# A conformer-like block with 32 experts on one core: the gating bias added by matmul instead of by VectorE, the convolution in eight columns per tap instead of four, one matmul group moved ahead of another

## The chip, the cores and the metric

The kernel runs on one core of a Trainium2 chip. The core's engines work side by side: TensorE (PE: matmuls; its weight loads are listed as PEld), VectorE (DVE), ScalarE (ACT), GpSimd (POOL), and SyncE (SP), which here only issues loads of weights. The metric is the device time of one execution in microseconds (us), lower is better.

## The reference

256 tokens of 1024 features pass through a first block and then through two layers of a second one. The change lies in the token mixer of the first block:

```
z = h @ w_in + b_in
a_val, a_gate, sgu, g_a, g_b = split(z)
ya = causal_depthwise_conv(a_val * sigmoid(a_gate), conv_w, conv_b)      # 31 taps per feature
ya = silu(layer_norm(ya)) @ w_a + b_a
u, v = split(gelu(sgu))
mixed = einsum('gij,bnjgc->bnigc', w, layer_norm(v)) + b_s[g, i]         # 8 groups, blocks of 128 tokens
yb = (u * mixed) @ w_b + b_b
y = (sigmoid(g_a) * ya + sigmoid(g_b) * yb) @ w_out + b_out
```

Behind it stand a layer norm, a mixture of 32 experts (4 per token, all 32 experts' weights are read), and the second block.

## The kernel before

**Tiles.** An activation that is feature-major has its features on the partitions as 8 columns `m` of 128, each with 256 tokens. It is held in `area`, which is cut into eleven pieces (`feat(i)`, `tok(i)`). A matmul group fills one of 8 PSUM banks; feature-major groups `q` = 0 to 3 hold columns 2q and 2q+1. Groups get their banks in turn, and a group's bank must have been emptied of the group that had it eight groups before. `G("mix", q)`, `G("w_b", q)`, `G("yaT", q)` and so on are such groups. The bank of `yaT` group q is that of `w_b` group q.

**Weights.** SP loads them in 1 MB units (1.05 MB decimal) in one fixed order, each into a slot of a ring; a load waits until the slot's earlier unit was used (semaphore `w_used`, counted by PE), and every later load waits behind it. PE reports the last use of a unit not at once but with the first matmul of the next step that calls `settle`. For the eighteen units of a_gate, a_val, u, g_a and the first half of g_b, ACT and DVE first split the weights into a high and a low part (L298 and L301), and PE makes three matmuls for one (L895, L897, L898); DVE's part of it is `early.below(n)`.

**Order on PE.** It is written out by hand: the first half of the modulation, transposes of h (`hT`), its second half, then a_gate, a_val, v and u with quarters of the second modulation (`mod2_0` to `mod2_3`) between them, g_a, the first half of g_b, the gating matmuls `mix` (L1061: 16 of 128 x 128 x 128), the second half of g_b (32 matmuls of 256 tokens, L857), the first half of w_b, the transposes `convT` (they wait for the whole convolution, `conv_ready`), the second half of w_b, the transposes `yaT` of the normed convolution, w_a, w_out, and then the experts. Before the first half of w_b PE waits until DVE has emptied all four `mix` groups.

**h in two parts.** ACT makes the high part and DVE the low part (L2029), two columns at a time with a tick of `h_low` each. a_gate's first half reads columns 0 to 3, and its second half columns 4 to 7.

**Order on DVE.** The convolution is 248 instructions of one column each: 8 that start the sums (L2055) and 240 multiply-adds (L2059). They run in two halves of four columns: first 31 taps for columns 0 to 3, then 31 for columns 4 to 7. In `for h in range(2 * TAPS)` each step is four instructions. Between the steps stand: the a_val product for columns 4 to 7 after 9 steps, the splits of units 8 and 9 after h = 24, those of units 10 to 17 at h = 34, 36, ..., 48, the modulation at h = 44, the layer norm of v after h = 48 (196 instructions done), and the gating products `mixed(q)` after h = 54 (220 done, 28 left). `mixed(q)` is two instructions on 128 x 512: L2065 adds b_s, which lies in `b_s_bc` on all partitions, and L2070 multiplies by u. The b_s load is a broadcast to 128 partitions, 512 KB, issued by ACT behind all other small loads.

**After the convolution.** DVE weighs w_b groups 0 and 1 with g_b (L2109), takes the moments of the transposed convolution, norms it (L1959), and waits for the router's and the experts' biases before it weighs w_b group 2. Those loads (`in_b_gu`, `in_b_dn`) are issued by POOL once `convT` and `mix` were emptied, behind the square root of the norm. Between the weighings of groups 2 and 3 DVE casts pieces of the bias (`bias_thirds`).

**Experts.** Sixteen 1 MB units are in the ring; the load of every unit after them waits for PE's use of the unit sixteen before it.

Of the kernel before, what the change touches and what calls it, by code (L numbers as in the profile page):

```python
# [9 lines left out]
ALU = mybir.AluOpType  # L10
# [3 lines left out]
P = 128  # L14
# [22 lines left out]
def build(nc, A, out):  # L37

    S, D = A["x"].shape[1], A["x"].shape[2]
    NT = S // P  # L40
# [19 lines left out]
    with ctx:  # L60
# [386 lines left out]
        b_s_in = sem("b_s_in")  # L447
# [7 lines left out]
        mix_biased = sem("mix_biased")  # L455
# [40 lines left out]
        b_s_bc = area[:, 10 * 2048 + 1024:11 * 2048].rearrange("p (g i) -> p g i", i=P)  # L496
# [325 lines left out]
        def _(pe):  # L822
# [83 lines left out]
            def feature_major_early(name, gname, xs, gi, x_half=lambda h: None):  # L906
                feature_major_parts(lambda h: early_unit(split_at[first_unit[name] + h]), gname, xs, gi, x_half)

            def feature_major_parts(unit_parts, gname, xs, gi, x_half=lambda h: None):

                gs = [G(gname, gi), G(gname, gi + 1)]
                for h in range(2):
                    x_half(h)
                    u = unit_parts(h)
                    for q in range(2):
                        if h == 0:
                            claim(pe, gs[q])
                        for m in range(2):
                            c = (2 * q + m) * P
                            for k in range(UK):  # L920
                                ins = three(bank(gs[q])[:, m * S:(m + 1) * S],
                                            parts_of(u, k, slice(c, c + P)),
                                            parts_of(xs, UK * h + k, slice(None)),
                                            h == 0 and m == 0 and k == 0, h == 1 and m == 1 and k == UK - 1)
                        if h == 1:
                            fills(ins, gs[q])
                    if h == 0:
                        ins.then_inc(w_used, 1)
                    else:
                        owed[0] = True  # L930
# [104 lines left out]
            feature_major_early("a_gate_0", "a_gate", h_parts, 0, lambda h: pe.wait_ge(h_low, 2 + 2 * h))  # L1035
# [5 lines left out]
            pe.wait_ge(rows_in, 48)  # L1041
# [9 lines left out]
            feature_major_early("g_b_0", "g_b", h_parts, 0)  # L1051
            pe.wait_ge(v_ready, NT)
            pe.wait_ge(wsT_ready, 1)
            vt = tok(4)
            for q in range(4):
                g = G("mix", q)
                claim(pe, g)
                for m in range(2):
                    gr = 2 * q + m
                    for t in range(NT):  # L1060
                        ins = mm(bank(g)[:, m * S + t * P:m * S + (t + 1) * P],  # L1061
                                 vt[:, t, gr * P:(gr + 1) * P], wsT[:, gr, :], start=True, stop=True)
                        settle(ins)
                fills(ins, g)
            feature_major("g_b_1", "g_b", hT, 1, first=1)
# [23 lines left out]
            pe.wait_ge(rows_in, 48)  # L1089
# [472 lines left out]
        def _(act):  # L1562
# [18 lines left out]
            for v in (A["b_a"][0], A["b_b"][0], A["b_out"][0]):  # L1581
# [6 lines left out]
            load(ws_raw, A["w_s"][0].rearrange("g i j -> i g j"), ws_in)  # L1588
            load(w_router[:, :, :], A["w_router"][0].rearrange("(k p) e -> p k e", p=P), rows_in)
# [6 lines left out]
            load(b_s_bc.rearrange("p g i -> p (g i)"),  # L1596
                 A["b_s"][0].rearrange("(o g) i -> o (g i)", o=1).to_broadcast([P, D]), b_s_in)
# [317 lines left out]
        def _(dve):  # L1915
# [118 lines left out]
            for q in range(4):  # L2034
                emptied(dve, G("a_gate", q))
            acc = feat(3)

            def value_half(c):
                for q in (2 * c, 2 * c + 1):
                    g = G("a_val", q)  # L2040
                    full(dve, g)
                    for m in range(2):
                        ins = v.scalar_tensor_tensor(apad[:, 2 * q + m, PADC:PADC + S],
                                                     bank(g)[:, m * S:(m + 1) * S], col("b_in", 2 * q + m),
                                                     feat(3)[:, 2 * q + m, :], ALU.add, ALU.mult)
                        if m == 0:
                            link(ins)
                    empties(ins, g)
                    emptied(dve, g)

            def taps(c, j):
                for i in range(4):
                    m, done = 4 * c + i, 4 * (TAPS * c + j) + i
                    if j == 0:
                        v.tensor_scalar(acc[:, m, :], apad[:, m, 0:S], col("conv_w", m), col("conv_b", m),  # L2055
                                        ALU.mult, ALU.add).then_inc(conv_step, 1)
                    else:
                        dve.wait_ge(conv_step, done - 3)
                        v.scalar_tensor_tensor(acc[:, m, :], apad[:, m, j:j + S], col("conv_w", j * ND + m),  # L2059
                                               acc[:, m, :], ALU.mult, ALU.add).then_inc(conv_step, 1)  # L2060

            def mixed(q):
                g = G("mix", q)
                full(dve, g)
                v.tensor_tensor(bank(g)[:, :].rearrange("p (m t i) -> p m t i", m=2, t=NT),  # L2065
                                bank(g)[:, :].rearrange("p (m t i) -> p m t i", m=2, t=NT),
                                b_s_bc[:, 2 * q:2 * q + 2, :].unsqueeze(2).to_broadcast([P, 2, NT, P]), ALU.add)\
                    .then_inc(mix_biased, 1)
                dve.wait_ge(mix_biased, q + 1)
                empties(v.tensor_tensor(feat(5)[:, 2 * q:2 * q + 2, :],  # L2070
                                        bank(g)[:, :].rearrange("p (m t) -> p m t", m=2),
                                        feat(5)[:, 2 * q:2 * q + 2, :], ALU.mult), g)

            value_half(0)
            for h in range(2 * TAPS):
                if h == 9:
                    value_half(1)
                taps(*divmod(h, TAPS))
                if h == 24:
                    early.below(10)  # L2080
                if 34 <= h <= 48 and h % 2 == 0:
                    early.below(11 + (h - 34) // 2)
                if h == 44:
                    for r in range(2):
                        mod_columns(G("mod2T", r), 1 + r)
                    v.tensor_scalar(sc2p[:, :], modc[:, 32:40], 1.0, None, ALU.add).then_inc(mod2_ready, 1)
                    dve.wait_ge(mod2_ready, 1)
                if h == 48:
# [4 lines left out]
                if h == 54:  # L2093
                    for q in range(4):
                        emptied(dve, G("u", q))
                    dve.wait_ge(b_s_in, 16)
                    for q in range(4):
                        mixed(q)
# [128 lines left out]
            dve.wait_ge(rows_in, 48)  # L2227
# [582 lines left out]
```

## Time and profile before

| | |
|---|---|
| median of 3 runs | 2157.81 us (2157.41 to 2160.37) |
| profiled execution | 2157.81 us, of which the span from first to last instruction is 2156.1 us |
| busy over the span | PE 91%, DVE 42%, ACT 21%, POOL 3% |
| 0 to 360 us, the stages up to the router | PE busy 303.69 us, DVE 236.91 us |
| 360 to 1380 us, the experts | PE busy 960.89 us, DMA share 0.93 |
| 1380 to 2156 us, the second block | PE busy 691.82 us, DVE 493.34 us |

A row of a timeline gives the start and the duration in us, the engine, the line, the operation, what it writes and reads, its shape and count, and in brackets how long the engine had been idle before it and what ended that. A matmul in f32 counts as two instructions. The durations of matmuls overlap; the distance of starts is what one costs. A row of a table by stretch gives for each engine the busy us and the number of instructions, then the granted clock of TensorE (1.00 is 2.4 GHz, 0.50 is 1.2 GHz), the busy share of the DMA engines and the GB/s moved.

### The profile page before, as it was taken

The page shows a single profiled execution, that of the slowest core. Times are in us where ns is not written, and L with a number is a line of the kernel's source. Part 1 is how long each engine was busy: PE and PEld are TensorE (multiplying, and loading weights), DVE is VectorE, ACT ScalarE, POOL GpSimd, SP SyncE. Part 2 cuts the span into 40 slices and gives each one's busy share as a digit, 9 for nine tenths or more (in the row PEclk, how much of TensorE's full clock was granted, in tenths as well). Part 3 has the DMA queues.
Part 4 walks back from the last instruction along what each step waited for, and adds up shares of the span by engine and source line. Part 5 has one row for each costly group of instructions (what it writes and reads, how often), then busy time and mean ns, then how long its engine had stood idle before and what let it go on. Part 6 is the DMA issues. An engine that isn't in the chain of part 4 may idle for free. (4 is left out here: it accounts for less than half of the span.)

```text
span 2156.1 us, 28523 instructions
## 1 busy us (share of the span) xinstructions
PE 1956.4 (91%) x10917; PEld 1229.7 (57%) x10918; DVE 914.4 (42%) x1463; ACT 456.6 (21%) x525; POOL 68.4 (3%) x123
## 2 busy tenths in 40 slices
PE   4999896999998989999988999779997898889997
PEld 2759764433333334333333343369986887868986
DVE  3799544111111111111111111366545887875554
ACT  2223101000000000000000000124532443324541
POOL 2000002000000000000000000000000000020000
PEclk9999997999999999999999999989999999999999
DMA  9694834959999999899999786464554420054551
GB/s 360 235 329 138 300 137 176 406 211 422 422 422 422 421 423 421 337 422 422 421 422 421 323 375 282 187 207 160 176 199 154 154 99 1 2 182 147 194 188 67
DMA packets 143588, 581.37 MB, mean 270 GB/s; under 512 B 10504, under 2 KB 12536, under 8 KB 94265
## 3 DMA queue, kind: packets, MB, share of 16 engines
q1 hardware_dynamic: 135824, 563.12, 67.1%
q0 software_dynamic: 3040, 11.02, 1.6%
q10 hardware_dynamic: 4649, 6.17, 0.8%
q8 instruction: 54, 0.88, 0.2%
q14 instruction: 21, 0.17, 0.0%
HBM read 579.23 MB, written 1.05 MB: 269 GB/s over the span
## 5 line engine op out<-in xcount | busy, mean ns | idle before, releaser
L1153 PE MATMUL bank<-ring,area 128*64 128x512 f32 x2048 | 461.4, 599 | 28.5 <-DMA ring<-in_w_gu 27.9
L1153 PEld LDWEIGHTS bank<-ring,area 128*64 128x64 f32 x2048 | 144.4, 137 | 327.6 <-issue 236.7
L895 PE MATMUL bank<-area_r,ring_r 128*128 128x256 f32 x992 | 284.6, 287 | 9.5 <-DVE area_r L2029 7.1
L897 PE MATMUL bank<-area_r,ring_r 128*128 128x256 f32 x992 | 282.9, 285 | 0.0
L898 PE MATMUL bank<-area_r,ring_r 128*128 128x256 f32 x992 | 282.8, 285 | 0.0
L288 DVE TENSOR_TENSOR ring_r<-ring,ring_r 128x2048 fp32r<-128x2048 f32 x90 | 206.1, 2292 | 176.6 <-ACT ring_r L285 176.1
L2297 DVE TENSOR_SCALAR area<-bank 128x512 f32<-128x512 f32 x36 | 24.9, 692 | 542.5 <-PE bank L1153 542.5
L285 ACT ACTIVATE ring_r<-ring 128x2048 fp32r<-128x2048 f32 x92 | 175.9, 1913 | 207.5 <-PE bank L898 188.8
L895 PEld LDWEIGHTS bank<-area_r,ring_r 128*128 128x128 f32 x992 | 192.8, 194 | 12.1 <-DVE area_r L2029 7.3
L1191 PE MATMUL bank<-area 128*64 128x512 f32 x864 | 192.5, 594 | 0.5 <-DVE area L2311 0.5
L897 PEld LDWEIGHTS bank<-area_r,ring_r 128*128 128x128 f32 x992 | 192.7, 194 | 0.5 <-issue 0.5
L898 PEld LDWEIGHTS bank<-area_r,ring_r 128*128 128x128 f32 x992 | 192.6, 194 | 0.0
L895 PE MATMUL bank<-ring_r,area_r 128*128 128x512 f32 x384 | 150.7, 392 | 5.0 <-DVE area_r L2176 5.0
L897 PE MATMUL bank<-ring_r,area_r 128*128 128x512 f32 x384 | 150.2, 391 | 0.0
L898 PE MATMUL bank<-ring_r,area_r 128*128 128x512 f32 x384 | 150.1, 391 | 0.0
L1699 ACT ACTIVATE area<-area 128x512 f32<-128x512 f32 x36 | 22.7, 630 | 536.1 <-DVE area L2297 536.1
L1191 PEld LDWEIGHTS bank<-area 128*64 128x64 f32 x864 | 62.6, 137 | 115.6 <-issue 111.9
L2059 DVE SCALAR_TENSOR_TENSOR area<-apad,cols,area 128x256 f32<-128x256 f32 x240 | 96.1, 478 | 0.3 <-DVE area L1976 0.2
L895 PEld LDWEIGHTS bank<-ring_r,area_r 128*128 128x128 f32 x384 | 72.5, 189 | 20.9 <-issue 4.7
L898 PEld LDWEIGHTS bank<-ring_r,area_r 128*128 128x128 f32 x384 | 72.5, 189 | 15.2
L897 PEld LDWEIGHTS bank<-ring_r,area_r 128*128 128x128 f32 x384 | 72.4, 189 | 14.8
L1126 PEld LDWEIGHTS bank<-area 128*128 128x128 f32 x544 | 64.8, 196 | 26.1 <-issue 13.9
(331 smaller groups left out, 2048.5 us busy)
## 6 DMA issues: line engine op xcount, KB each, us to landing
ring<-in_w_gu SPq DMA_DIRECT2D x256, 1024.0 KB, 21.2
area<-in_w_dn SPq DMA_DIRECT2D x96, 1024.0 KB, 21.5
ring<-in_mlp_w SPq DMA_DIRECT2D x64, 1024.0 KB, 5.4
ring<-in_w_dn SPq DMA_DIRECT2D x32, 1024.0 KB, 19.9
ring<-in_w_in SPq DMA_DIRECT2D x24, 1024.0 KB, 6.2
ring<-in_gdn_w_in SPq DMA_DIRECT2D x16, 1024.0 KB, 5.5
area<-in_w_mod SPq DMA_DIRECT2D x12, 1024.0 KB, 8.8
ring<-in_w_mod SPq DMA_DIRECT2D x8, 1024.0 KB, 17.2
```

Source lines behind the costliest of these rows:

```text
L285: nc.scalar.activation(unit_high(i), raw, ACT.Copy).then_inc(w_high, 1)
L288: nc.vector.tensor_tensor(unit_low(i), raw, unit_high(i), ALU.subtract).then_inc(w_split, 1)
L895: ins = mm(out_, a_[0], b_[0], start=start, stop=False)
L897: mm(out_, a_[0], b_[1], start=False, stop=False)
L898: return mm(out_, a_[1], b_[0], start=False, stop=stop)
L1126: ins = mm(bk[:, d * P:(d + 1) * P], h2_tok[:, t, (UK * dh + d) * P:(UK * dh + d + 1) * P], slots[:, t, :], start=t == 0, stop=t == NT - 1)
L1153: ins = mm(bk[hf * BLK:(hf + 1) * BLK, :], x(kt), block_u[:, c:c + BANK], start=False, stop=kt == ND - 1)
L1191: ins = mm(bT[hf * BLK:(hf + 1) * BLK, :], actT[:, 2 * i + k, fh * BLK:(fh + 1) * BLK], block_u[:, c:c + BANK], start=n == 0 and k == 0, s ...
L1699: f(g_sig, g_min, ACT.Sigmoid, scale=SWIGLU).then_inc(moe_act, 1)
L2059: v.scalar_tensor_tensor(acc[:, m, :], apad[:, m, j:j + S], col("conv_w", j * ND + m), acc[:, m, :], ALU.mult, ALU.add).then_inc(conv_step, 1)
L2297: step(v.tensor_scalar(g_min, banks[5][:, :], LIMIT, None, ALU.min))
```

## The change

It does five things.

1. a_gate's first half no longer starts when two ticks of `h_low` are there; it waits for all four.
2. b_s is loaded as one row on one partition (4 KB, `b_s_row`), ahead of the router's weights in ACT's queue; the 512 KB broadcast goes. The semaphores that count the rows count one more.
3. The second half of g_b stands before the `mix` matmuls on PE instead of behind them.
4. Each of the 16 `mix` outputs gets a second matmul ahead of its own: ones (1 partition x 128) times b_s_row (1 x 128), accumulated in the same bank. DVE's four additions L2065 go. In the `mix` loop nothing calls `settle` any more, so the last use of g_b's second unit is reported by w_b's first matmul.
5. The convolution runs tap by tap over all eight columns. All of a_val is multiplied before it begins. Steps are now eight instructions: splits 8 and 9 after j = 7, splits 10 to 17 after j = 11 to 18, the modulation after j = 16, the layer norm of v after j = 18 (152 instructions done), the gating products after j = 24 (200 done, 48 left).

```diff
-            feature_major_early("a_gate_0", "a_gate", h_parts, 0, lambda h: pe.wait_ge(h_low, 2 + 2 * h))
+            pe.wait_ge(h_low, 4)
+            feature_major_early("a_gate_0", "a_gate", h_parts, 0)
...
             feature_major_early("g_b_0", "g_b", h_parts, 0)
+            feature_major("g_b_1", "g_b", hT, 1, first=1)
+
             pe.wait_ge(v_ready, NT)
             pe.wait_ge(wsT_ready, 1)
...
-                        ins = mm(bank(g)[:, m * S + t * P:m * S + (t + 1) * P],
-                                 vt[:, t, gr * P:(gr + 1) * P], wsT[:, gr, :], start=True, stop=True)
-                        settle(ins)
+                        o = bank(g)[:, m * S + t * P:m * S + (t + 1) * P]
+                        mm(o, ones[0:1, :], b_s_row[0:1, gr * P:(gr + 1) * P], start=True, stop=False)
+                        ins = mm(o, vt[:, t, gr * P:(gr + 1) * P], wsT[:, gr, :], start=False, stop=True)
                 fills(ins, g)
-            feature_major("g_b_1", "g_b", hT, 1, first=1)
...
+            load(b_s_row, A["b_s"][0].rearrange("(o g) i -> o (g i)", o=1), rows_in)
...
-            load(b_s_bc.rearrange("p g i -> p (g i)"),
-                 A["b_s"][0].rearrange("(o g) i -> o (g i)", o=1).to_broadcast([P, D]), b_s_in)
...
-            value_half(0)
-            for h in range(2 * TAPS):
-                if h == 9:
-                    value_half(1)
-                taps(*divmod(h, TAPS))
-                if h == 24:
+            for m in range(ND):
+                v.tensor_scalar(acc[:, m, :], apad[:, m, 0:S], col("conv_w", m), col("conv_b", m),
+                                ALU.mult, ALU.add).then_inc(conv_step, 1)
+            for j in range(1, TAPS):
+                for m in range(ND):
+
+                    dve.wait_ge(conv_step, j * ND + (m + 1 - ND))
+                    v.scalar_tensor_tensor(acc[:, m, :], apad[:, m, j:j + S], col("conv_w", j * ND + m), acc[:, m, :],
+                                           ALU.mult, ALU.add).then_inc(conv_step, 1)
+                if j == 7:
                     early.below(10)
-                if 34 <= h <= 48 and h % 2 == 0:
-                    early.below(11 + (h - 34) // 2)
-                if h == 44:
+                if 11 <= j <= 18:
+                    early.below(j)
+                if j == 16:
...
-                if h == 48:
+                if j == 18:
...
-                if h == 54:
+                if j == 24:
...
-                    dve.wait_ge(b_s_in, 16)
                     for q in range(4):
-                        mixed(q)
+                        g = G("mix", q)
+                        full(dve, g)
+                        empties(v.tensor_tensor(feat(5)[:, 2 * q:2 * q + 2, :],
+                                                bank(g)[:, :].rearrange("p (m t) -> p m t", m=2),
+                                                feat(5)[:, 2 * q:2 * q + 2, :], ALU.mult), g)
```

## Rows read from the trace of the kernel before

**Rows 1.** Busy time by stretch: the first stages, then the experts.

```profile
0.00:360.00 360.00, 303.69 (x1765) 235.05 (x1766) 236.91 (x453) 78.58 (x103) 36.92 (x94) 0.94 0.68 239
360.00:1380.00 1020.00, 960.89 (x4712) 372.46 (x4712) 184.15 (x464) 87.71 (x140) 0.00 (x0) 0.99 0.93 384
```

**Rows 2.** Timeline of PE, 32 to 46 us: second half of mod1, its transposes, a_gate's first.

```profile
32.99 3.64 PE L1009 MATMUL bank<-ring,cond 128*32 128x512 f32 x32 [1.92 <-DMA ring<-in_w_mod]
37.40 0.66 PE L836 MATMUL bank<-ident,area 128*128 128x128 f32 x4 [0.77 <-ACT area L1601]
45.11 0.58 PE L895 MATMUL bank<-area_r,ring_r 128*128 128x256 f32 x1 [7.06 <-DVE area_r L2029]
```

**Rows 3.** Timeline of DVE, 44 to 49 us: second and fourth tick of h_low.

```profile
44.37 0.69 DVE L2029 TENSOR_TENSOR area_r<-area,area_r 128x512 fp32r<-128x512 f32 x1
...
47.89 0.69 DVE L2029 TENSOR_TENSOR area_r<-area,area_r 128x512 fp32r<-128x512 f32 x1
```

**Rows 4.** ACT's issue of the b_s broadcast: KB each, us to landing.

```profile
17.27 0.35 ACTq L1572 DMA_DIRECT2D area<-in_b_s  x1
...
area<-in_b_s ACTq DMA_DIRECT2D x1, 512.0 KB, 12.4
```

**Rows 5.** Timeline of PE, 113 to 122 us: matmuls with one partition, then with 128.

```profile
113.82 1.12 PE L874 MATMUL bank<-area,ones 1*128 1x512 f32 x2
114.87 7.13 PE L877 MATMUL bank<-ring,area 128*128 128x512 f32 x16
121.93 0.63 PE L1009 MATMUL bank<-area,cond 128*32 128x512 f32 x3
```

**Rows 6.** Timeline of DVE, 99 to 226 us: taps, a split, gating products.

```profile
99.50 25.42 DVE L2059 SCALAR_TENSOR_TENSOR area<-apad,cols,area 128x256 f32<-128x256 f32 x64
...
147.95 2.29 DVE L301 TENSOR_TENSOR ring_r<-ring,ring_r 128x2048 fp32r<-128x2048 f32 x1
...
200.04 9.59 DVE L2059 SCALAR_TENSOR_TENSOR area<-apad,cols,area 128x256 f32<-128x256 f32 x24 [0.25 <-DVE area L1976]
209.55 0.69 DVE L2065 TENSOR_TENSOR bank<-bank,area 128x512 f32<-128x512 f32 x1
...
214.88 11.16 DVE L2059 SCALAR_TENSOR_TENSOR area<-apad,cols,area 128x256 f32<-128x256 f32 x28
```

**Rows 7.** Timeline of PE, 203 to 292 us: mix, g_b and w_b, convT, yaT, w_a.

```profile
203.86 3.74 PE L1061 MATMUL bank<-area 128*128 128x128 f32 x32
207.44 7.93 PE L857 MATMUL bank<-area,ring 128*128 128x256 f32 x36
...
235.07 1.91 PE L836 MATMUL bank<-ident,area 128*128 128x128 f32 x16
...
250.63 0.60 PE L971 MATMUL bank<-ident,area 128*128 128x128 f32 x4
...
256.31 2.39 PE L971 MATMUL bank<-ident,area 128*128 128x128 f32 x10 [1.91 <-DVE area L2109]
261.53 29.87 PE L857 MATMUL bank<-area,ring 128*128 128x256 f32 x128 [2.83 <-issue]
291.24 3.73 PE L1081 MATMUL bank<-apad,ones 128*128 128x128 f32 x32
```

**Rows 8.** POOL's issue of the experts' biases, and DVE's weighing behind their landing.

```profile
242.57 1.84 POOL L747 DMA_DIRECT2D area<-in_b_gu  x3 [0.42 <-issue]
...
252.91 1.00 DVE L2109 SCALAR_TENSOR_TENSOR area<-bank,cols,area 128x256 f32<-128x256 f32 x2 [6.05 <-DMA area<-in_b_dn]
```

**Rows 9.** Busy time by stretch: within w_b's second half, and w_a's start.

```profile
244.00:250.00 6.00, 6.00 (x30) 5.28 (x29) 2.86 (x15) 0.00 (x0) 0.89 (x2) 1.00 1.05 307
...
262.00:263.00 1.00, 1.00 (x4) 0.73 (x4) 0.00 (x0) 0.00 (x0) 0.37 (x1) 0.50 0.83 344
```

**Rows 10.** SP's load queue: its waits from 360 to 1400 us, and an issue.

```profile
SPq L662 <- PE bank L1153: 435.9, 194, 33.0
...
367.78 13.58 SPq L662 DMA_DIRECT2D ring<-in_w_gu  x8
```

More of the change, by code:

```diff
@@ L446, in build @@
         b_out_in = sem("b_out_in")
-        b_s_in = sem("b_s_in")
         g1_ready = sem("g1_ready")
@@ L454, in build @@
         conv_step = sem("conv_step")
-        mix_biased = sem("mix_biased")
         cond_ready = sem("cond_ready")
@@ L495, in build @@
         PACK_ROWS = (128, 3 * ND, 96, 128, TAPS * ND - 128)
-        b_s_bc = area[:, 10 * 2048 + 1024:11 * 2048].rearrange("p (g i) -> p g i", i=P)
+        b_s_row = area[0:1, 10 * 2048 + 1024:11 * 2048]
         ws_raw, wsT = half(9, 0), half(9, 1)
@@ L904, in feature_major_late, with feature_major_early, feature_major_parts @@
                 feature_major_parts(lambda h: late_unit(LATE[name] + 2 * slab + h), gname, xs, gi)
-            def feature_major_early(name, gname, xs, gi, x_half=lambda h: None):
-                feature_major_parts(lambda h: early_unit(split_at[first_unit[name] + h]), gname, xs, gi, x_half)
-            def feature_major_parts(unit_parts, gname, xs, gi, x_half=lambda h: None):
+            def feature_major_early(name, gname, xs, gi):
+                feature_major_parts(lambda h: early_unit(split_at[first_unit[name] + h]), gname, xs, gi)
+            def feature_major_parts(unit_parts, gname, xs, gi):
                 gs = [G(gname, gi), G(gname, gi + 1)]
                 for h in range(2):
-                    x_half(h)
                     u = unit_parts(h)
@@ L1040, in _ @@
             mod2_part(1)
-            pe.wait_ge(rows_in, 48)
+            pe.wait_ge(rows_in, 64)
             token_major("v_0", "v", tokens_of(hT), 1, bias=row8)
@@ L1088, in _ @@
             h2T = feat(1)
-            pe.wait_ge(rows_in, 48)
+            pe.wait_ge(rows_in, 64)
             g = G("router")
@@ L2035, in _ @@
                 emptied(dve, G("a_gate", q))
-            acc = feat(3)
[L2038 to L2072, printed above, removed]
@@ L2074, in _ @@
-            value_half(0)
-            for h in range(2 * TAPS):
-                if h == 9:
-                    value_half(1)
-                taps(*divmod(h, TAPS))
-                if h == 24:
+            for q in range(4):
+                g = G("a_val", q)
+                full(dve, g)
+                for m in range(2):
+                    ins = v.scalar_tensor_tensor(apad[:, 2 * q + m, PADC:PADC + S], bank(g)[:, m * S:(m + 1) * S],
+                                                 col("b_in", 2 * q + m), feat(3)[:, 2 * q + m, :], ALU.add, ALU.mult)
+                    if m == 0:
+                        link(ins)
+                empties(ins, g)
+                emptied(dve, g)
@@ L2092, in _ @@
                     layer_norm(tok(4), v_ready)
-                if h == 54:
+                if j == 24:
                     for q in range(4):
                         emptied(dve, G("u", q))
-                    dve.wait_ge(b_s_in, 16)
                     for q in range(4):
-                        mixed(q)
+                        g = G("mix", q)
+                        full(dve, g)
+                        empties(v.tensor_tensor(feat(5)[:, 2 * q:2 * q + 2, :],
+                                                bank(g)[:, :].rearrange("p (m t) -> p m t", m=2),
+                                                feat(5)[:, 2 * q:2 * q + 2, :], ALU.mult), g)
                     tick(areas_free)
@@ L2226, in _ @@
             full(dve, g)
-            dve.wait_ge(rows_in, 48)
+            dve.wait_ge(rows_in, 64)
             L = R["logits"]
```

## The prediction

> **What bounds the kernel now.** I read the busy time by stretch first. The change lies in the first 360 us, where PE is busy 84% and DVE 66% [rows 1]. Nothing there is bound by one engine throughout, so the timelines of PE and DVE, laid side by side, decide. On PE's from 203 to 292 us the reader is to see that it hardly stops until the transposes yaT: mix at 203.86, g_b's second half at 207.44, w_b's first half, convT at 235.07, all without an idle bracket [rows 7]. On DVE's, that it is in step with PE, not ahead of it: the last gating product follows 209.55 plus four pairs of instructions, about 215, and the last 28 taps end at 214.88 + 11.16 = 226.04 [rows 6]. PE wants the products at w_b's start and the whole convolution at convT. The g_b half and the w_b half are 128 instructions in 235.07 - 207.44 = 27.63 us, so 0.216 us each and 13.8 us a half [rows 7]; w_b starts at 221.3. The slack is thus 6.3 us for the products and 9.0 us for the convolution. Behind it the experts' stretch has a DMA share of 0.93 [rows 1], but its load queue is opened by PE: SP waits 435.9 us for PE's expert matmuls and issues the first load past the filled ring at 367.78, when PE has begun [rows 10]. So I take a shift of PE's arrival there as a shift of the end.
>
> **a_gate waits for all of h.** PE starts at 45.11, right behind the second tick at 44.37 + 0.69 = 45.06; the fourth comes at 47.89 + 0.69 = 48.58 [rows 2, 3]. Start: +3.5 us. The splits it then needs are made by ACT and DVE in the same rhythm, and the a_gate and a_val loops free their slots by PE's progress, so nothing catches up; the delay stays. TensorE's clock had already fallen in the 7.06 us of idle time [rows 2], so I charge nothing for three more.
>
> **The b_s load.** 512 KB leave the DMA engines; they were issued at 17.27 and landed 12.4 us later, at 29.7, before the modulation weights for which PE waited 1.92 us until 32.99 [rows 2, 4]. At the 384 GB/s of rows 1 that is 0.52 MB / 384 = 1.4 us of DMA time. PE's idle 1.92 us covers it, and from there the chain runs through to h_low. I take -1.4 us (ends: 0 if the weights' queue didn't yield to it, -1.9). The Trainium skill, "DMA: Bandwidth & Descriptors", Queues, rings and completion order, says that each DMA engine takes turns between its queues packet by packet; by that, bytes of ACT's queue that land earlier than the weights were taken from the weights' time, as I assumed. Net start: +2.1 us.
>
> **The bias matmuls.** 16 more matmuls are 32 more instructions on PE, with nothing beside them. The trace has none of 1 x 128 on 1 x 128. Nearest rows: mix itself costs (207.44 - 203.86) / 16 = 0.224 us, so 16 cost at least 3.6 us [rows 7]. A one-partition matmul of 512 columns, followed by a 128-partition one, costs 114.87 - 113.82 = 1.05 us, where one of 128 partitions costs (121.93 - 114.87) / 8 = 0.88 [rows 5]: 0.17 us more for going from one shape to the other. The change does this sixteen times. I take 0.224 + 0.17 = 0.39 each, 6.3 us. Ends: 3.6 us with no switching cost, 16.8 us if each costs the full 1.05; a gain is excluded, since the instructions are only added to an engine that takes them in order. The Trainium skill, "TensorEngine Tiling (Array Packing)", Key Properties, says that changing the tiling mode drains TensorE. Rows 5 agree as to the sign, with 0.17 us. Without the rule and without the switch the sum would be 2.7 us smaller.
>
> **The convolution and the order of g_b and mix.** Up to the norm of v, DVE's stops are the same splits at the same distance of eight taps; at 147.95 it takes a split without a wait [rows 6], and with the change it will stand there waiting for ACT, with fewer taps done. It has done 152 of 248 instructions after that norm instead of 196. Its loss of 44 is no loss until the tail. One tap costs 25.42 / 64 = 0.397 us [rows 6].
> - Norm of v done: 199.8 (its successor starts at 200.04 after 0.25 idle, [rows 6]) + 2.1 = 201.9. 48 taps to the products, 19.1 us: DVE stands at mix at 221.0.
> - PE reaches the end of g_b's first half at 203.86 + 2.1 = 206.0, g_b's second half ends at 219.8, mix with its bias takes 3.6 + 6.3 = 9.9 us: 229.7, the four groups each 2.5 us apart, the first at 222.3. DVE is there in time for the first and then waits for PE.
> - PE stands still for the last product: semaphore and one instruction of 0.69 us, about 0.9 us. This was covered by g_b's second half before. w_b starts at 230.6 and is half done at 244.4.
> - DVE goes on at 230.5 with 48 taps instead of 28: 19.1 us, 249.6. The cover of 13.8 us is too short: PE waits 5.2 us for `conv_ready`. convT at 249.6 instead of 235.07, +14.5.
>
> The four additions L2065 that DVE loses (0.69 us each, [rows 6]) gain nothing on this path, since DVE then waits for PE. g_b's second half isn't late for ACT's sigmoids; w_b needs them 10 us later.
>
> **The clock.** PE full on, 244 to 250 us had the clock 1.00; after the idle pieces around yaT w_a starts at 0.50 [rows 9]. w_a takes 291.24 - 261.53 = 29.7 us for 128 instructions, against 27.6 at the full clock [rows 7]: 2.1 us lost. The new wait of 5.2 us is as long as those pieces together, so I charge the same, +2.1, at convT and w_b's second half (ends: 0 and 2.7).
>
> **yaT gives some back.** Before, from convT to w_b's end are 250.63 - 235.07 = 15.6 us; from there to w_a 10.9 us [rows 7], because DVE's weighing of group 2 waited until 252.91 for the experts' biases, issued at 242.57, 7.5 us behind convT's start, and still landing ten us later [rows 8]. Now w_b's second half ends at 249.6 + 15.6 + 2.1 = 267.3. The biases are issued at 257.1 and, if it takes the same ten us, would be there at 267.4. I expect them some us sooner: with `settle` gone, the queue goes on at 230.6 and nine units of 1.05 MB at 384 GB/s take 24.6 us, to 255, and the experts' first loads wait for w_b's use, near 266. So group 3 is weighed right behind w_b's end, 1.2 us after it, and from there the rest is as before, 261.53 - 256.31 = 5.2 us. 6.4 instead of 10.9: -4.5 us. If the landing takes its ten us, the second weighing, two casts and the third push this out by about 3. w_a, which waits for units loaded behind `settle`, needs them at 274; covered by 30 us.
>
> **Sum.** +2.1 +6.3 +0.9 +5.2 +2.1 -4.5 = +12.1 us. The profiled execution took 2157.81 us, which is also the median, so no correction: 2169.9 us. A measurement of this kernel tells about 0.2%, 4.3 us, from no change.
>
> **Rivals.**
> - *The small bill.* One-partition matmuls switch at no cost (-2.7) and the clock doesn't fall in the 5.2 us (-2.1): 2165.1. For it: a lone wait may be too short for the clock. Against it: rows 5, and rows 9. Chance 0.2; it lies within the range of my forecast.
> - *The big bill.* Each one-partition matmul costs 1.05 us whatever its columns: +10.5, 2180.4. Chance 0.04. Or the biases' landing takes ten us again, and b_s gives nothing back: +3 +1.4, 2174.3. Chance 0.12.
> - *The tail stays covered.* DVE gets the products done 5.2 us sooner relative to w_b's start, so PE doesn't wait at convT and the clock stays; 2169.9 - 5.2 - 2.1 = 2162.6. It would need mix to be later than DVE, that is a DVE that isn't held at mix. Against it: the product can't be made before PE's matmuls, and 48 taps at 0.397 us outlast 64 instructions at 0.216 wherever both start together. Chance 0.06.
> - *The other side: the experts take it up.* If the experts' stretch were timed by its loads alone and they started no later, the 12.1 us would vanish in it: not slower, 2157.8, or 2156.4 if only b_s's bytes count. It decides as soon as the loads' start doesn't move with PE. For it: DMA share 0.93. Against it: the ring is full and quiet before 367.78, and the queue waits for PE [rows 10]. Chance 0.08, of which 0.03 for faster.
>
> **The numbers.** The forecast itself, 2166 to 2174, has 0.5. The range takes in the small bill and the first part of the big one: 2162.5 to 2176. Slower by over 0.2% (over 2162.1): 0.5 + 0.2 + 0.16 + 0.04 of the 0.06 = 0.9, which I cut to 0.88 for what I don't see; within 0.2%: 0.08; faster: 0.04.
>
> **What would show it.** a_gate's first instruction at about 47.2. mod1's second half at about 31.6. mix's 64 instructions over some 10 us (7 if switching is free). DVE idle between groups at the products. PE idle of about 0.9 us ahead of w_b and of about 5 us ahead of convT, put down to DVE's taps, and a granted clock of 0.5 behind it. w_a starting 6 to 7 us after w_b's end. The experts' stretch as long as before. The prediction is wrong if the wait ahead of convT is missing, if mix takes over 15 us, or if the experts' stretch shrinks by what the stages before it lose.

## The result and the profile after

The changed kernel takes 2176.5 us (median of 4 runs, 2172.49 to 2181.28), the kernel before 2158.89 in the 4 runs beside it (2157.41 to 2160.37), 17.6 us less. Over all 31 executions of the changed kernel (median 2178.5) the ratio is 1.0091, 95% interval 1.0075 to 1.0107, about 19.6 us slower. The forecast was 12.1 us slower, 2169.9, with a range up to 2176.0: the direction was right, the size wrong. The profiled execution after took 2173.47 us, among the fastest of the 31; its span is 2171.7 us, 15.6 more than before.

PE's timeline after, from the second half of mod1 to the experts, at the places of [rows 2] and [rows 7]:

```profile
31.77 4.62 PE L1006 MATMUL bank<-ring,cond 128*32 128x512 f32 x32 [0.41 <-DMA ring<-in_w_mod]
37.19 0.66 PE L834 MATMUL bank<-ident,area 128*128 128x128 f32 x4 [0.79 <-ACT area L1599]
48.43 0.58 PE L893 MATMUL bank<-area_r,ring_r 128*128 128x256 f32 x1 [10.59 <-DVE area_r L2027]
...
205.75 9.45 PE L855 MATMUL bank<-area,ring 128*128 128x256 f32 x43
...
219.66 0.48 PE L1062 MATMUL bank<-area,ones 1*128 1x128 f32 x2
220.08 0.49 PE L1063 MATMUL bank<-area 128*128 128x128 f32 x2
220.50 0.48 PE L1062 MATMUL bank<-area,ones 1*128 1x128 f32 x2
...
225.13 0.80 PE L1063 MATMUL bank<-area 128*128 128x128 f32 x2
225.85 0.79 PE L1062 MATMUL bank<-area,ones 1*128 1x128 f32 x2
226.57 0.80 PE L1063 MATMUL bank<-area 128*128 128x128 f32 x2
...
238.15 0.80 PE L1063 MATMUL bank<-area 128*128 128x128 f32 x2
239.99 5.46 PE L855 MATMUL bank<-area,ring 128*128 128x256 f32 x12 [1.05 <-issue]
...
258.78 3.43 PE L834 MATMUL bank<-ident,area 128*128 128x128 f32 x16 [2.06 <-DVEq L1983]
262.00 8.19 PE L855 MATMUL bank<-area,ring 128*128 128x256 f32 x36
...
276.07 0.82 PE L968 MATMUL bank<-ident,area 128*128 128x128 f32 x6
277.43 1.31 PE L968 MATMUL bank<-ident,area 128*128 128x128 f32 x10 [0.55 <-DVE area L2088]
282.20 29.55 PE L855 MATMUL bank<-area,ring 128*128 128x256 f32 x128 [3.46 <-issue]
311.59 3.73 PE L1080 MATMUL bank<-apad,ones 128*128 128x128 f32 x32
```

The lines have moved: L855 is L857 of before, L1063 is L1061, L1062 is the bias. Read down the starts. a_gate is 3.3 us late, g_b's second half starts 1.9 us after the place where mix stood, mix itself begins at 219.66, where it was expected (219.8), and then takes until 238.9: 19.2 us, against 3.6 before and 9.9 expected. From 219.66 a pair of bias and mix takes 220.50 - 219.66 = 0.84 us (0.83 over the first six). From 225.13 on it takes 226.57 - 225.13 = 1.44. What stands behind it, the stop of 1.05 us ahead of w_b, a wait for the taps ahead of convT, the short stop at yaT and 3.46 us of idle time ahead of w_a, is there in the order foreseen and about 9 us later; only the wait ahead of convT is 2.06 us and not 5.2.

The windows show why a pair gets slower on the way: the last column but two is the granted clock, and it falls to half while PE is without a pause.

```profile
218.00:222.00 4.00, 4.00 (x21) 2.91 (x19) 3.03 (x8) 0.84 (x2) 0.00 (x0) 1.00 0.61 224
222.00:226.00 4.00, 4.00 (x19) 2.75 (x18) 0.69 (x1) 0.00 (x0) 0.00 (x0) 0.87 0.10 38
226.00:230.00 4.00, 4.00 (x12) 2.84 (x12) 0.69 (x1) 0.00 (x0) 0.00 (x0) 0.50 0.00 0
```

DVE's timeline after, at the place of [rows 6], has it waiting at each of the four products, and then 48 taps:

```profile
201.94 19.09 DVE L2053 SCALAR_TENSOR_TENSOR area<-apad,cols,area 128x256 f32<-128x256 f32 x48 [0.25 <-DVE area L1974]
223.20 0.69 DVE L2075 TENSOR_TENSOR area<-bank,area 128x512 f32<-128x512 f32 x1 [2.17 <-PE bank L1063]
...
238.98 0.69 DVE L2075 TENSOR_TENSOR area<-bank,area 128x512 f32<-128x512 f32 x1 [5.09 <-PE bank L1063]
239.59 19.08 DVE L2053 SCALAR_TENSOR_TENSOR area<-apad,cols,area 128x256 f32<-128x256 f32 x48
```

### The profile page after: what moved, and what is told of

Its sections match the earlier page's. It is cut to its first block and busy times, and to the rows that moved or that the text cites. A ratio compares the mean times of both kernels' runs of the same rounds, so it can differ in the third digit from the quotient of the medians.

```text
span 2171.7 us, 28581 instructions
## 1 busy us (share of the span) xinstructions
PE 1971.4 (91%) x10949; PEld 1240.0 (57%) x10950; DVE 911.8 (42%) x1459; ACT 457.0 (21%) x525; POOL 68.4 (3%) x123
## 3 DMA queue, kind: packets, MB, share of 16 engines
HBM read 578.71 MB, written 1.05 MB: 267 GB/s over the span
## 5 line engine op out<-in xcount | busy, mean ns | idle before, releaser
L893 PEld LDWEIGHTS bank<-area_r,ring_r 128*128 128x128 f32 x992 | 192.9, 194 | 15.6 <-DVE area_r L2027 10.8
L893 PEld LDWEIGHTS bank<-ring_r,area_r 128*128 128x128 f32 x384 | 72.1, 188 | 20.5 <-issue 4.6
## 6 DMA issues: line engine op xcount, KB each, us to landing
ring<-in_w_dn SPq DMA_DIRECT2D x32, 1024.0 KB, 19.6
```

What stands on the lines that cost most here:

```text
L893: ins = mm(out_, a_[0], b_[0], start=start, stop=False)
```

## The experiments

Each ratio is to runs of the kernel before on the same chip, with its 95% interval.

**e1_dve_bias.** The changed kernel with the bias on VectorE as before; it differs from the kernel before by a_gate's wait, the taps and the order.

```diff
-                        mm(o, ones[0:1, :], b_s_row[0:1, gr * P:(gr + 1) * P], start=True, stop=False)
-                        ins = mm(o, vt[:, t, gr * P:(gr + 1) * P], wsT[:, gr, :], start=False, stop=True)
+                        ins = mm(o, vt[:, t, gr * P:(gr + 1) * P], wsT[:, gr, :], start=True, stop=True)
```

> This is the changed kernel with the bias of the gating given back to VectorE (the 512 KB broadcast of b_s and the four additions as in the kernel before); a_gate's wait, the order of g_b and mix and the taps are the changed ones. Theory A (the sixteen one-partition matmuls are the mis-sized term: in the changed kernel's trace mix takes 20 us instead of 3.6, 0.83 us a pair at the full clock and 1.45 at half): mix is back at 3.6 us at the full clock, the last product is done near 226.5, the taps near 245.6, PE waits about 5 us ahead of convT, and w_a starts 8 us later than before: +8 us, ratio to before 1.0037. Rival B (the clock falls there for another reason, the long stretch with DVE's products on the path): mix is still slow and the ratio stays at 1.007 or above.

Measured 1.0043 (1.003 to 1.0057). PE's timeline of this run, mix and what follows it:

```profile
220.69 3.73 PE L1062 MATMUL bank<-area 128*128 128x128 f32 x32
227.79 1.62 PE L857 MATMUL bank<-area,ring 128*128 128x256 f32 x3 [3.37 <-issue]
```

Mix is back at 3.6 us. PE then waits 3.37 us for DVE, which comes to the products at 222.06 and needs 5.3 us for four additions and four products. Ahead of convT it waits 1.70 us, not the 5 expected, for w_b's half took 17.09 us instead of 14 (granted clock 0.50 from 228 to 232 us). w_a starts 7.3 us late, 8 were expected. So the taps, the order and a_gate's wait make about half of the loss, and the bias on PE the other half: 1.0091 against 1.0043, 10 us. Theory A holds and rival B falls.

**e2_bias_only.** The kernel before with only the bias changed: b_s as a row, and the sixteen one-partition matmuls in the `mix` loop.

```diff
-                        ins = mm(bank(g)[:, m * S + t * P:m * S + (t + 1) * P],
-                                 vt[:, t, gr * P:(gr + 1) * P], wsT[:, gr, :], start=True, stop=True)
+                        settle(mm(o, ones[0:1, :], b_s_row[0:1, gr * P:(gr + 1) * P], start=True, stop=False))
+                        ins = mm(o, vt[:, t, gr * P:(gr + 1) * P], wsT[:, gr, :], start=False, stop=True)
```

> The kernel before with the bias by sixteen one-partition matmuls and b_s as one row, nothing else. Theory A: mix takes 13 us at the full clock and up to 20 if the clock falls in it, all of it on PE's path, and the convolution's end (226) stays covered: +10 to +18 us, ratio 1.0045 to 1.008. Rival C (the bias matmuls cost this much only because DVE's tail stands behind them): about +3.6 us for the bare instructions, ratio 1.002.

Measured 1.0102 (1.0087 to 1.0116), above what I expected, and in time not less than the whole change. PE's timeline in this run, and a window behind it:

```profile
202.65 0.48 PE L1060 MATMUL bank<-area,ones 1*128 1x128 f32 x2
203.06 0.49 PE L1061 MATMUL bank<-area 128*128 128x128 f32 x2
203.48 0.48 PE L1060 MATMUL bank<-area,ones 1*128 1x128 f32 x2
```

```profile
206.00:210.00 4.00, 4.00 (x13) 2.88 (x12) 2.93 (x7) 0.00 (x0) 0.00 (x0) 0.50 0.01 2
```

Again 0.83 us a pair, and the clock falls 3.3 us after the first pair. Mix goes on to 223.19, 20.5 us. Here all of it is added to PE's path; the taps end under it and give nothing back, and the stops at yaT stay. w_a starts at 278.86, 17.3 us late, which is inside what I expected. The other 5 us of the span came behind w_a, where this profile has falls of the clock that the one of before has not (0.61 from 1862 to 1870 us, for one). Rival C falls.

The parts don't add up to the whole. At w_a they are 7.3 us (e1) and 17.3 (e2), 24.6 together, and the whole change is 20.7 late. Of the 3.9 us between, 2.3 are PE's stop for the products, 3.37 us in e1 and 1.05 in the whole change, where DVE has no additions to make and follows the longer mix group by group; 1.3 us are the mix, whose clock fell later in the profile after than in e2. The give-back at yaT is no part of the difference: e1 has it too (6.7 us from w_b's end to w_a instead of 10.9).

**e3_bias_128 and e12_bias_128_again.** The changed kernel with as many bias matmuls of as many columns, but on 128 partitions.

```diff
-                        mm(o, ones[0:1, :], b_s_row[0:1, gr * P:(gr + 1) * P], start=True, stop=False)
+                        mm(o, ident[:, 0:1].to_broadcast([P, P]), b_s_bc[:, gr * P:(gr + 1) * P], start=True, stop=False)
```

> The changed kernel with each of the sixteen bias matmuls on 128 partitions instead of one: the stationary operand is the identity's first column spread over 128 columns, the moving one b_s broadcast to all partitions (the 512 KB load is back, ahead of the router's weights). Same count of instructions, same columns. Theory A1 (going from one partition to 128 and back is what costs): a pair takes 0.45 us, mix 7.2 us, no fall of the clock; +9 us over before, ratio 1.0042. Rival A2 (the number of matmuls costs, whatever their rows): a pair takes 0.83 us as in the changed kernel, ratio 1.008 or above.

> The kernel of e3 once more, for its times spread from 2161 to 2177 us. Theory A: a pair takes 0.446 us again, mix 7.1 us; against the run with the bias on VectorE (1.0043) the added 3.6 us of matmuls make 1.006, and where the time lies above 2172 the granted clock has fallen somewhere on the way (in mix, w_b or w_a). Rival A2: a slower mix in this profile.

Measured 1.0063 (1.0042 to 1.0083) and 1.0046 (1.0029 to 1.0063). PE's timeline of e3:

```profile
220.52 0.38 PE L1062 MATMUL bank<-area,ident 128*128 128x128 f32 x2
220.74 0.39 PE L1063 MATMUL bank<-area 128*128 128x128 f32 x2
220.96 0.39 PE L1062 MATMUL bank<-area,ident 128*128 128x128 f32 x2
...
227.44 0.39 PE L1063 MATMUL bank<-area 128*128 128x128 f32 x2
228.88 0.45 PE L855 MATMUL bank<-area,ring 128*128 128x256 f32 x1 [1.05 <-issue]
```

A pair takes 220.96 - 220.52 = 0.44 us, mix 7.1, and the clock was 1.00 throughout it, in both runs (e12's mix also took 7.1). So 64 instructions cost 7 us here and 19 when every other matmul has one partition; the rows, not the count, make the difference, and A2 falls. What I expected of the spread, that a fall of the clock elsewhere accounts for runs above 2172 us, is borne out in part only: from w_b's second half to the transposes yaT, e12's profile (span 2171.5 us) needs 1.3 us more than e3's (2162.7), and in w_a 30.3 against 29.4. The other 6.7 us between the two spans lie behind w_a. The clock goes the same way there: its mean over the span is 0.965 in e12 and 0.971 in e3, and at one place, 1853 to 1862 us, e12 has 0.62 where e3 has no fall. I haven't placed all of it.

**e4_bias_wide.** The changed kernel with one one-partition matmul of 512 columns for each bank.

```diff
+                mm(bank(g)[:, :], ones[0:1, :],
+                   b_s_row[0:1, 2 * q * P:2 * (q + 1) * P].rearrange("o (m i) -> o m i", m=2)
+                   .unsqueeze(2).to_broadcast([1, 2, NT, P]), start=True, stop=False)
```

> The changed kernel with four one-partition matmuls of 512 columns, one for each bank, in place of sixteen of 128. Theory A1: four switches there and back and 4 x 1.05 us, mix 4.2 + 3.6 = 7.8 us, ratio to before 1.0045. Rival A2 (cost by columns only): the same columns as before, so mix stays at 13 us at the full clock or 20 with a fall.

Measured 1.0068 (1.0052 to 1.0084). PE's timeline:

```profile
220.03 1.12 PE L1058 MATMUL bank<-area,ones 1*128 1x512 f32 x2
221.09 1.16 PE L1065 MATMUL bank<-area 128*128 128x128 f32 x8
222.17 1.12 PE L1058 MATMUL bank<-area,ones 1*128 1x512 f32 x2
```

A bank takes 2.14 us, mix 8.5; expected were 7.8 us and a ratio of 1.0045, so both are missed, and A2, which wanted 13 us or more, falls. w_a starts at 270.96, where e3 has 270.78. Four matmuls of the mix behind the wide one take 1.08 us, where [rows 7] give 4 x 0.224 = 0.90. So 0.18 us hang on the way back, besides the 0.19 on the one-partition matmul itself. That is what my reading of [rows 5] missed (below). The clock stayed up through this mix, with a matmul of one partition in each bank, and fell only behind the stop ahead of w_b:

```profile
224.00:229.00 5.00, 4.66 (x24) 2.71 (x22) 1.68 (x3) 0.00 (x0) 0.00 (x0) 1.00 0.00 0
229.00:232.00 3.00, 2.29 (x6) 1.87 (x7) 3.00 (x8) 0.00 (x0) 0.00 (x0) 0.59 0.08 6
```

**e11_bias_grouped.** As e2, but four bias matmuls and then four of mix for each bank.

```diff
+                for m in range(2):
+                    for t in range(NT):
+                        settle(mm(bank(g)[:, m * S + t * P:m * S + (t + 1) * P], ones[0:1, :],
+                                  b_s_row[0:1, (2 * q + m) * P:(2 * q + m + 1) * P], start=m == 0 and t == 0,
+                                  stop=False))
                 for m in range(2):
```

> The kernel before with the sixteen one-partition bias matmuls of 128 columns, but four at a time: for each bank four bias matmuls and then its four mix matmuls. Same instructions and columns as e2_bias_only, four changes of shape there and back instead of sixteen. Theory A1 (each way there and back costs 0.38 us at the full clock): 32 x 0.224 + 4 x 0.38 = 8.7 us for mix instead of 13.3, less if the one-partition matmuls overlap, and a smaller chance that the clock falls: ratio 1.003. Rival A3 (every one-partition matmul of 128 columns costs 0.42 us by itself): 13 us at the full clock, ratio as e2, 1.01.

Measured 1.0042 (1.0024 to 1.006), against 1.0102 for e2, with the same instructions in another order. PE's timeline, and a window behind the fall of the clock:

```profile
202.26 1.15 PE L1058 MATMUL bank<-area,ones 1*128 1x128 f32 x8
203.35 1.16 PE L1064 MATMUL bank<-area 128*128 128x128 f32 x8
204.43 1.17 PE L1058 MATMUL bank<-area,ones 1*128 1x128 f32 x8
205.53 2.08 PE L1064 MATMUL bank<-area 128*128 128x128 f32 x8
```

```profile
206.00:208.00 2.00, 2.00 (x10) 1.77 (x10) 2.00 (x6) 0.00 (x0) 0.00 (x0) 0.50 0.01 4
```

Four and four take 2.17 us at the full clock, 0.38 more than 8 x 0.224. One way there and back costs 0.38, whether it has one matmul of 128 columns on each side (0.83 - 0.45), four, or a wide one (2.14 - 0.86 - 0.90). A3 falls. The clock fell in this profile too, so mix took 13.2 us instead of the 8.7 expected. Its twelve runs spread from 2155.9 to 2174.4 us, and the mean granted clock goes with them: the four up to 2161.1 us have 0.972 or 0.973, the eight from 2165.5 us on 0.962 to 0.969. Whether it is the fall in the mix that the four lack isn't shown; the one profile is of a run of the eight.

**e5_h_low.** The kernel before with a_gate waiting for the fourth tick.

```diff
-            feature_major_early("a_gate_0", "a_gate", h_parts, 0, lambda h: pe.wait_ge(h_low, 2 + 2 * h))
+            feature_major_early("a_gate_0", "a_gate", h_parts, 0, lambda h: pe.wait_ge(h_low, 4))
```

> The kernel before with a_gate waiting for all four ticks of h_low, nothing else. Theory A: PE starts at 48.6 instead of 45.1 and nothing catches up; the experts' start and the end are 3.5 us later, ratio 1.0016. Rival D (the later start is taken up at a later stop, the one for the modulation's weights at 100 us or the one for the experts' biases at 253): ratio 1.000.

Measured 1.0014 (1.0001 to 1.0026), 3.0 us. a_gate starts at 48.55, and mix at 206.56, 2.7 us late. Rival D lies just outside the interval; that w_a too is 3.0 us late (264.56) speaks against it.

**e6_taps, e7_g_b_first, e8_taps_g_b_first.** The kernel before with the convolution loop of the change, with `feature_major("g_b_1", ...)` ahead of mix, and with both; the additions stay.

```diff
+            for j in range(1, TAPS):
+                for m in range(ND):
...
+            feature_major("g_b_1", "g_b", hT, 1, first=1)
             pe.wait_ge(v_ready, NT)
```

> The kernel before with the taps over eight columns, and the a_val products ahead of them; mix stays ahead of g_b's second half, the bias stays on VectorE. Theory A: VectorE comes to the products at 219 instead of 209.5, ends them at 224.5, the 48 taps left end at 243.7, PE waits 3 us ahead of w_b and 5 ahead of convT: convT at 243.8, +8.7; the clock takes 2 more, the stop at yaT gives 4.5 back: +6 us, ratio 1.003. Rival E (the tail is covered as before): ratio 1.000.

> The kernel before with g_b's second half ahead of mix, nothing else. Theory A: PE waits for the last product, about 1.5 us with its addition, the 28 taps end near 234, ahead of w_b's half: +1.5 us, ratio 1.0007. Rival F (the order alone uncovers the convolution): ratio 1.002 or above.

> The kernel before with both the taps over eight columns and g_b's second half ahead of mix; the bias stays on VectorE and a_gate starts at the second tick. Theory A: VectorE's taps set convT in both orders, so the same as the taps alone within 1 us: +6 us, ratio 1.003; with a_gate's 3.5 us it makes the run with the bias on VectorE (1.0043). Rival F: the two add up, 1.004 or more.

Measured 1.0021 (1.0005 to 1.0036), 0.9994 (0.998 to 1.0008) and 1.0018 (1.0005 to 1.0032): the taps cost 4.5 us where 6 were expected, the order nothing that shows in the time, and both together what the taps cost. E and F fall, E only just by the interval, but the stops in the trace settle it. PE's timeline of e6, w_b and convT:

```profile
226.17 14.05 PE L857 MATMUL bank<-area,ring 128*128 128x256 f32 x64 [3.37 <-issue]
...
244.97 1.34 PE L836 MATMUL bank<-ident,area 128*128 128x128 f32 x6 [4.74 <-DVEq L1985]
```

The stops are those worked out: 3 us for the products (3.37), 5 for the taps (4.74). The row of e7 shows that the order isn't free where it stands:

```profile
223.78 16.95 PE L857 MATMUL bank<-area,ring 128*128 128x256 f32 x64 [3.19 <-issue]
```

PE waits 3.19 us for the last addition and product (1.5 were expected), w_b's half then takes 17 us with the clock at 0.50 (223 to 227 us), and convT starts at 240.57, 5.5 us late. From w_b's end to w_a it is 6.4 us instead of 10.9, so w_a is only 1.0 us late: the wait for the experts' biases takes the order's cost up.

**e9_best and e10_early_bias.** The stop at yaT, which the prediction used as a give-back, was there in the kernel before, so it could be had without the change. e10 lets POOL issue the experts' biases before the root it waits for; e9 also has ACT issue the b_s broadcast after h's high part.

```diff
             load_norm(1)
-            norm_root()

             for e in range(4):
                 emptied(pool, G("convT", e))
                 emptied(pool, G("mix", e))
-            load(*[(bgu_raw[NE * r:NE * (r + 1), :], A["b_gu"][0]) for r in range(3)],
-                 (b_dn_sb, A["b_dn"][0]))
+            for dst, src in [(bgu_raw[NE * r:NE * (r + 1), :], A["b_gu"][0]) for r in range(3)] + \
+                    [(b_dn_sb, A["b_dn"][0])]:
+                late[0] += 16
+                pool.dma_start(dst, src).then_inc(late_in, 16)
+            norm_root()
+            pool.wait_ge(late_in, late[0])
```

> A version that might beat both: the kernel before, with GpSimd issuing the experts' biases as soon as convT and mix were emptied, ahead of the square root of the convolution's norm instead of behind it, and with the broadcast of b_s issued by ScalarE behind h's high part, out of the modulation weights' way. Theory A: the biases are issued 3 to 4.5 us earlier, VectorE's weighing of w_b group 2 and the transposes yaT move up by as much, and mod1's second half starts 1.0 us earlier (as it did in the runs without the broadcast): -4.5 us, ratio 0.998. Rival G (the landing is set by the weights' queue in front of it, the DMA engines being full from 234 to 254 us): the biases land as late as before, ratio 0.9995.

> The first half of e9 alone: the biases' loads issued ahead of the root, b_s as in the kernel before. Theory A: w_a starts 3 to 4 us earlier, ratio 0.9985. Rival G: ratio 1.000, w_a where it was.

Measured 0.9967 (0.9951 to 0.9983) and 0.9976 (0.996 to 0.9992): 7 and 5 us faster than the kernel before. The timeline of e9, with mod1 and a_gate at the places of [rows 2], POOL's issue and DVE's weighing at those of [rows 8], and w_a:

```profile
31.64 3.64 PE L1012 MATMUL bank<-ring,cond 128*32 128x512 f32 x32 [0.50 <-DMA ring<-in_w_mod]
...
43.77 0.58 PE L898 MATMUL bank<-area_r,ring_r 128*128 128x256 f32 x1 [7.06 <-DVE area_r L2032]
...
235.93 0.52 POOL L761 DMA_DIRECT2D area<-in_b_gu  x1 [37.11 <-ACT area L1672]
...
246.95 1.01 DVE L2112 SCALAR_TENSOR_TENSOR area<-bank,cols,area 128x256 f32<-128x256 f32 x2 [2.62 <-DMA area<-in_b_dn]
...
255.12 1.19 PE L860 MATMUL bank<-area,ring 128*128 128x256 f32 x2 [3.45 <-issue]
```

w_a starts at 255.12 instead of 261.53; in e10 at 257.17. The last of the biases is issued 6.7 us earlier in e9 (4.7 in e10) and DVE's weighing behind its landing is 6.0 us earlier (3.9), so the full DMA queues did not hold it back as rival G had it (from issue to landing it took 9.2 us in e9, 9.3 in e10 and 8.5 in the kernel before). The difference between e9 and e10 in a_gate's start is 45.09 - 43.77 = 1.3 us; in the time it is within the intervals.

## Why the prediction was wrong in size

**a_gate's wait**: right. Alone it puts a_gate's start 3.4 us later (e5, 48.55 against 45.11) and costs 3.0 us in time; 3.5 were foreseen.

**The b_s load**: the mechanism was right, its use not always there. Without the broadcast, mod1's second half starts at 31.77 instead of 32.99, and in e2 and e4, which have only the row, a_gate started 1.0 us earlier than in the kernels of the same order that have the broadcast (44.04 against 45.11, 47.68 against 48.64). In the profiled run after, the clock was at half for part of that half of mod1 (0.77 from 31 to 37 us; 4.62 us for what took 3.64), and the gain was gone but for 0.2 us at 37.19. That isn't the row's doing: in e6 and e8, which load the broadcast, the same half took 5.56 and 5.87 us. The net start of +2.1 came out at 3.3, and then at 1.9 by 205.75, because in this execution the clock didn't fall behind the stop at 104 us, as it had in the one before at 101.7: the window 103 to 105 us had 0.50 before and 1.00 after. That 1.9 is so near to the 2.1 foreseen is luck.

**The bias matmuls**: this is the term that failed. I charged 6.3 us; mix took 19.2 instead of 3.6, which is 15.6, and the prediction had named over 15 us for mix as a sign that it is wrong. Two things were missing.
- The switch. I took 0.17 us from [rows 5] by comparing the one-partition matmul with the sixteen instructions right behind it. Those carry the way back. The row to compare with is w_out's in the trace of before, whose first half has no one-partition matmul ahead of it:

```profile
294.81 13.90 PE L877 MATMUL bank<-ring,area 128*128 128x512 f32 x32
308.54 13.90 PE L877 MATMUL bank<-area 128*128 128x512 f32 x32
```

  That is (308.54 - 294.81) / 16 = 0.858 us for a matmul of 512 columns. By this, [rows 5] give 1.05 - 0.86 = 0.19 on the one and 7.06 - 8 x 0.858 = 0.20 on the others, together 0.39 us for there and back. It was in the trace. 16 x (0.224 + 0.38) = 9.7 us, 3.4 more than I charged; the runs e4 and e11 confirm 0.38. The Trainium skill, "TensorEngine Tiling (Array Packing)", Key Properties, says that a change of tiling mode drains TensorE. Taken as such a change, the way from 128 partitions to one and back agrees with it, at 0.38 us, and e3, which keeps 128 partitions, has none of it.
- The clock. I charged no fall inside mix, since PE is never idle there. It fell to half 5.0 us after the first pair in the changed kernel (3.3 in e2, under 4 in e11), each time while matmuls of 128 columns with one partition ran among the others, and not in the same columns on 128 partitions (e3, e12), nor with four matmuls of 512 columns on one partition (e4). 19.2 - 16 x 0.83 = 5.9 us. So three profiles with one-partition matmuls of 128 columns have the fall, and two with the same columns on 128 partitions have none; why that is, and why e4 has none, stays open.

**The tail of the convolution**: right. PE's stop for the last product was 1.05 us (0.9 foreseen). The wait ahead of convT was 2.06 instead of 5.2, because the clock, still at half behind mix, made w_b's half slower; that took from the wait and did not move convT, which the 48 taps set. With the bias on VectorE, in e6, the wait was 4.74. From the last product to convT 19.1 us were foreseen and 19.2 measured (239.59 to 258.78).

**The clock behind convT and yaT's give-back**: right. convT and w_b's half took 17.3 us (17.7 foreseen), and from there to w_a 6.1 (6.4 foreseen, 10.9 before).

**From w_a to the end**: the shift stays. w_a begins 282.20 - 261.53 = 20.7 us late in the profiles, and the experts' first matmuls are still 20.7 late (383.92 against 363.26). The span grew by only 15.6. The code behind is the same, and 3.4 of these 5 us go with the clock. Behind the experts the profile of before has a fall that the other has not (0.57 from 1412 to 1416 us, against 1.00 from 1431 to 1435), first the row before and then the same row after:

```profile
1412.50 8.83 PE L1289 MATMUL bank<-area 128*128 128x256 f32 x32 [3.02 <-DVE area L2376]
1431.44 7.17 PE L1288 MATMUL bank<-area 128*128 128x256 f32 x32 [2.07 <-DVE area L2355]
```

That is 1.7 us, and the same again near 1935 us (0.76 from 1930 to 1940, against 0.97 from 1948 to 1958). The other 1.6 us went within the experts. The profile after is also a fast one of its kernel (2173.47 us, the median 2178.5), so the 19.6 us of the ratio are the better measure. Runs of the kernel before alone spread over 2147 to 2165 us.

The sum with the measured bias in place of the 6.3 us would have been 12.1 + 3.4 + 5.9 = 21.4 us, against 20.7 at w_a in the profile and 19.6 by the ratio. What was also wrong is the range: for the bias I had named 16.8 us as its upper end, by the full price of a wide matmul, and given that case 0.04, since I took the nearer row for the better one. That this end lies near the measured 15.6 is luck: no one-partition matmul of 128 columns took 1.05 us; at the full clock the sixteen cost 9.7, and the rest is the clock.

## What to carry to other kernels

A one-partition matmul that adds a bias isn't priced by its columns alone: each way from 128 partitions to one and back costs, 0.38 us here, so put the bias matmuls of several outputs together (e11), or leave the bias on an engine where other work covers it, as VectorE's additions were in the kernel before. When a price is taken as the difference of two rows, take the second from a place that the effect can't reach, not from the neighbour. When two engines meet twice, the work between the meetings on the later one must be covered by what the other has in between; here 48 taps against one half of w_b. And a step that costs nothing in time may be covered by a stop further on, as e7's order was by the wait at yaT.

## What was not expected of the hardware

The granted clock fell from 2.4 to 1.2 GHz while the trace shows no idle time on PE, in a run of small matmuls that alternated between one partition and 128 (19.2 us of mix, full clock for the first 5), and came back only in w_b's first half. The same stop doesn't always bring a fall: behind 2.85 us of idle time at 100 us the clock fell in the profile before, and behind 2.95 us at 104 us it did not in the one after. A change from 128 partitions to one and back costs 0.38 us whether the matmuls between have 128 or 512 columns. A load on GpSimd's queue, issued while the DMA engines were full of weights (share 1.05), landed 8.5 to 9.3 us after its issue in the kernel before, e9 and e10, whenever that was, and 4.3 us after it in the changed kernel, where the share was down to 0.73.
